# Which products of the second attention run as split fp32r, and which engine makes their weight remainders

## The chip, the cores and the metric

One core of one Trainium2 chip runs the whole program. The metric is the device time of one execution in microseconds; lower is better. The median of three runs of the kernel before is 2136.24 us (2134.52 to 2136.61).

## What is computed

The reference is a chain of two blocks on 256 tokens of width 1024, in fp32: a first block (sparse attention, latent attention, cross attention to a memory, a mixture of experts), then a second block of two layers. Layer 0 is a state-space mixer and a mixture of experts over the tokens and a context of 256 rows. Layer 1 is the part that is changed here and what follows it:

```python
h = rmsnorm(x, norm1_w) * (1 + sc1) + sh1          # tokens and context, each with its own scale and shift
q, k, v = split(h @ qkv_w)                          # 16 query heads, 4 key heads, 4 value heads of 64
q, k = rmsnorm per head, 2-D rotary embedding on the tokens
o = softmax(q @ concat(k_tokens, k_context).T / 8) @ v          # 256 x 1024
x = x + g1 * (o @ out_w)                                        # out_w is 1024 x 1024
x = x + g2 * moe_ec(rmsnorm(x, norm2_w) * (1 + sc2) + sh2)      # 16 experts, each takes 32 tokens; w1, w3, w2 are 1024 x 1024
return rmsnorm(x, final_norm_w)
```

The weights of the last mixture are 16 experts x 3 matrices x 4 MiB, 201 MB that are read from HBM once.

## The kernel before, in words

**Engines and queues.** Every engine has its own instruction stream, written out by hand in blocks (`@block.tensor`, `@block.scalar`, `@block.vector`, `@block.gpsimd`, `@block.sync`), and runs it strictly in order; they meet in semaphores (`wait_ge`, `then_inc`). The functions of one stage are five such lists. PSUM's eight banks are handed out in turn (`banks.open`); each bank is emptied by VectorE (`DVE`) or ScalarE (`ACTE`).

**Weights.** All weights come through a ring of pieces of 2 MiB (`weights`, `Ring`, `load_weights`). SBUF has seven slots (0 to 6) and some further rooms that are used in layer 1's mixture: the room of the queries and of `C` (slot number `SLOTS + 2`), an extra tile (`SLOTS + 1`), and the upper half of `hT` with another tile (`SLOTS + 3`). SyncE issues the loads in the order of the list, and before each it waits until the piece that held the slot before has been used (`before.freed`). `ring.add(name, slot, 0)` reserves a slot without a load: it is used for the rounded copy of a weight piece. The list order is: six pieces per expert of layer 0's mixture, the three pieces of the attention's qkv weight (`("qkv", 0..2)` in slots 6, 5, 4), the two pieces of its out-projection (slots 0 and 6), and six pieces per expert of layer 1's mixture in a cycle of ten places (line 378).

**Split products.** A plain fp32 matmul is exact enough but slow. `matmul_split` (lines 563 to 567) takes both operands as a sum of a rounded part (type fp32r) and a remainder, and issues three fp32r matmuls: high by low, high by high, low by high. The rounding is an ScalarE copy into an fp32r tile, the remainder a VectorE subtraction of the rounded tile from the original.

**The second attention (lines 3557 to 3800).** ScalarE rounds qkv piece 0, takes the squares of the four row tiles (two of context, two of tokens), rounds piece 1. GpSimd makes the four reciprocal roots, VectorE scales the rows, TensorE transposes them, and both VectorE and ScalarE evict the transposed rows into `hT` with scale and shift (`evict_h`). ScalarE then rounds `hT` into `h_high` in 16 parts of 256 columns, first the tokens' half, then the context's; VectorE makes the remainders `h_low` (`lower_h`) and those of the weights (`lower_w`), which go back into the slots of the raw weights. All three qkv pieces are multiplied as split products: pieces 0 and 1 for the queries (two row tiles each), piece 2 for keys and values (four row tiles). VectorE normalises and rotates the queries in four units (`QU`) and then the keys in four units, with reciprocal roots by GpSimd between; the remainders of piece 2 stand between the query units.

Then `PairAttention` (lines 982 to 1074) goes through eight pairs of heads, two steps each: TensorE the logits, VectorE the maximum, ScalarE the exponential with the sum, VectorE the scaling, TensorE the transposes, ScalarE their copies (`pT`), TensorE the products with the values (`pv`). VectorE copies each pair's output from PSUM into `oT` (line 1050). The out-projection (line 3657) is a plain fp32 matmul over `oT`, 32 products of 128 x 128 by 128 x 512, first the half `h = 0` of the weight for all four output tiles, then `h = 1`.

**The last mixture (`expert_choice(1)`).** After the norm and the routing, TensorE goes through the experts piece by piece (line 3217). A piece's place is free again when TensorE has used it; the piece ten places later in the list can then be loaded.

Of the kernel before, what the change touches and what calls it, by code (L numbers as in the profile page):

```python
# [5 lines left out]
F32 = mybir.dt.float32  # L6
# [175 lines left out]
def build(nc, A, out):  # L182
# [11 lines left out]
    with ctx:  # L194
# [183 lines left out]
        moe2_weights(1, (3, 5, 1, 4, SLOTS + 2, 2, SLOTS + 1, 0, 6, SLOTS + 3))  # L378
# [605 lines left out]
        class PairAttention:  # L984
# [4 lines left out]
            def __init__(self, tag, pairs, qT, kT, v, scale, outT, bufs):  # L989
                self.tag, self.steps, self.qT, self.kT, self.v = tag, 2 * pairs, qT, kT, v  # L990
                self.scale, self.outT = scale, outT
# [39 lines left out]
            def vector(self, dve, link):  # L1031
                for s in range(self.steps + self.LAG + 2):
# [13 lines left out]
                    p = self.done_pair(s - self.LAG - 1)  # L1046
                    if p is not None:
                        o = banks[self.tag, "pv", p]
                        dve.wait_ge(bank_full, o.full)
                        dve.tensor_copy(self.outT(p), o.ap[:, 0:S]).then_inc(emptied[DVE], 1)  # L1050

            def scalar(self, act):
                for s in range(self.steps + self.LAG):
                    if s < self.steps:
                        for i in (2 * s, 2 * s + 1):
                            act.wait_ge(self.max_ready, i + 1)
                            if i >= self.RING:
# [3 lines left out]
                                           accum_out=self.sums[:, i:i + 1]).then_inc(emptied[ACTE], 1)  # L1061
                    m = s - self.LAG
                    if m >= 0:
# [1992 lines left out]
        def expert_choice(l):  # L3056
# [11 lines left out]
            with ExitStack() as scope:  # L3068
# [41 lines left out]
                for n, piece in enumerate(PIECES):  # L3110
                    e, j = divmod(n, 6)
                    piece.freed = (half_used, 3 * e + j // 2 + 1) if j % 2 == 0 else ((h1_full, h3_full, y_full)[j // 2], e + 1)
                    if l == 0 and n % 8 == 7 or l == 1 and n % 10 == 6:
                        piece.ap = extra[0][:, :]
                    if l == 1 and n % 10 == 4:
# [440 lines left out]
        with ExitStack() as scope:  # L3556
# [3 lines left out]
            h_low = hT_r  # L3560
            h5_rounded, h5_split, w5_rounded, w5_split = (sem(x) for x in ("h5_rounded", "h5_split", "w5_rounded", "w5_split"))
            QKV = [(ring["qkv", n], ring["qkv_high", n]) for n in range(3)]
# [5 lines left out]
            early = ring["moe2", 1, 4]  # L3568
# [14 lines left out]
            oT = hflat[:, 0:2048].rearrange("p (k n) -> p k n", k=8)  # L3583
# [12 lines left out]
                                lambda p, kt: vv[:, kt, kv_of(p) * 64:(kv_of(p) + 1) * 64], HD ** -0.5, lambda p: oT[:, p, :], bufs)  # L3596
            block = whole

            def rounded_qkv(n, low=False):
                return rounded_slot(QKV[n][0 if low else 1].slot).rearrange("p (k n) -> p k n", k=KD)  # L3600

# [4 lines left out]
            def _(pe):  # L3606
                def product(tag, n, at, steps):
                    b = banks.open(tag, ACTE)
                    pe.wait_ge(*b.emptied)
                    for k in range(KD):  # L3610
                        if steps is not None:
                            pe.wait_ge(h5_split, steps + k)
# [237 lines left out]
```

## Time and profile before

| | |
|---|---|
| median of 3 runs | 2136.24 us |
| the profiled execution | 2135.01 us |
| its span (first to last instruction) | 2133.1 us |
| TensorE busy | 1980.8 us, 93% |
| VectorE / ScalarE / GpSimd busy | 952.6 / 682.2 / 98.1 us |
| DMA | 623.61 MB, mean 292 GB/s |
| granted TensorE clock | 0.982 of full speed, mean |

The profile is one execution. A plain fp32 matmul shows as two records of a matmul each, so 32 products are 64 records. "PE" is TensorE, "DVE" VectorE, "ACT" ScalarE, "POOL" GpSimd, "SPq" the queue of SyncE that issues the loads. A view of stages gives for each stretch how long every engine was busy; the chain of waits goes back from the last instruction to whatever released it and is printed in order of time; a timeline lists instructions of one engine, equal ones merged. Times are microseconds from the start of the span.

The attention of layer 1 lies between about 1503 and 1663 us, the last mixture behind it.

### The profile page before, as it was taken

What the parts mean: (1) busy time and instruction counts of PE and PEld (TensorE: products, weight loads), DVE (VectorE), ACT (ScalarE), POOL (GpSimd) and SP (SyncE); (2) the same over time, 40 slices, a digit from 0 to 9 for tenths busy, and PEclk for the clock granted to TensorE, in tenths of its full rate; (3) what the DMA queues carried; (4) which work ended last, traced back from release to release, by engine and by line L of the source; (5) the groups of instructions that cost most, each with busy time, mean ns of one, the idle gap of its engine ahead of it and who ended that gap; (6) DMA issues with size and microseconds to landing.
All of it is one profiled execution on the core that took longest, in us unless ns stands there. A gap on an engine that the chain in (4) does not pass through costs nothing.

```text
span 2133.1 us, 24870 instructions
## 1 busy us (share of the span) xinstructions
PE 1980.8 (93%) x10092; PEld 1088.3 (51%) x10092; DVE 952.6 (45%) x1702; ACT 682.2 (32%) x1326; POOL 98.1 (5%) x105
## 2 busy tenths in 40 slices
PE   8988988999899999999899999988899899999887
PEld 6845654444578888878533333322564433333222
DVE  5667425454887888853612222212875401111101
ACT  5254313111577776752311111100544211111001
POOL 0101000000101000100000000000210000000000
PEclk9989989999999999999999999999999999999999
DMA  9637778999044334325599999999641599999997
GB/s 368 218 126 276 285 290 319 383 404 334 25 141 119 100 118 144 113 73 218 206 422 428 427 427 428 427 427 426 262 183 60 216 418 425 428 426 426 426 427 323
DMA packets 143378, 623.61 MB, mean 292 GB/s; under 512 B 10976, under 2 KB 61280, under 8 KB 105376
## 3 DMA queue, kind: packets, MB, share of 16 engines
q1 hardware_dynamic: 141104, 618.83, 72.9%
q10 hardware_dynamic: 2160, 3.18, 0.4%
q8 instruction: 81, 1.33, 0.3%
q14 instruction: 33, 0.27, 0.0%
HBM read 620.80 MB, written 1.18 MB: 292 GB/s over the span
## 4 chain that ended last, share of the span: by engine, by line
PE 72%; DMA 14%; DVE 7%; ACT 3%; issue 2%; POOL 1%; SPq 1%; DVEq 0%; POOLq 0%; ACTq 0%
PE bank L3217 21%; PE bank L565 8%; PE bank L567 7%; PE bank L566 7%; DMA slots<-in_moe_w 7%; PE bank L1973 4%; DMA extra0e<-in_moe_w 3%; PE bank L635 2%; PE bank L3238 2%; PE bank L2000 2%; DMA hT<-in_moe_w 2%; PE bank L3188 2%; DMA spare_slot<-in_attn_qkv_w 2%; PE bank L2515 1%; PE bank L3657 1%
## 5 line engine op out<-in xcount | busy, mean ns | idle before, releaser
L3217 PE MATMUL bank<-slots,xgTe 128*64 128x512 f32 (+1 forms) x1408 | 315.6, 594 | 27.3 <-DMA slots<-in_moe_w 27.3
L3487 DVE TENSOR_TENSOR actse<-sge,bank 32x512 f32<-32x512 f32 (+1 forms) x48 | 32.8, 683 | 500.4 <-PE bank L3217 272.0
L3217 PEld LDWEIGHTS bank<-slots,xgTe 128*64 128x64 f32 (+1 forms) x1408 | 94.4, 124 | 229.2 <-issue 193.6
L3380 ACT ACTIVATE sge<-bank 32x512 f32<-32x512 f32 (+1 forms) x48 | 28.4, 591 | 461.2 <-PE bank L3217 461.0
L3217 PE MATMUL bank<-slots,aTe 128*64 128x512 f32 (+1 forms) x688 | 156.9, 601 | 13.6 <-issue 12.5
L566 PE MATMUL bank<-slots_r 128*128 128x512 f32 x416 | 163.4, 393 | 0.0
L565 PE MATMUL bank<-hT_r,slots_r 128*128 128x512 f32 x384 | 155.6, 405 | 0.0
L567 PE MATMUL bank<-slots_r 128*128 128x512 f32 x384 | 152.1, 396 | 0.0
L3392 ACT ACTIVATE aTe<-bank 128x512 f32<-128x512 f32 x32 | 19.1, 597 | 284.6 <-PE bank L3291 284.6
L2420 DVE TENSOR_TENSOR slots_r<-slots,slots_r 128x2048 fp32r<-128x2048 f32 x32 | 76.6, 2395 | 68.2 <-ACT slots_r L2415 68.1
L3217 PEld LDWEIGHTS bank<-slots,aTe 128*64 128x64 f32 (+1 forms) x688 | 49.8, 126 | 105.4 <-issue 103.1
L2792 DVE SCALAR_TENSOR_TENSOR slots<-slots,columns 128x512 f32<-128x512 f32 x128 | 98.7, 776 | 4.1 <-ACT slots L2637 0.3
L1973 PE MATMUL bank<-slots,hT 128*64 128x512 f32 x320 | 85.0, 595 | 4.9 <-ACT hT L2085 4.9
L566 PEld LDWEIGHTS bank<-slots_r 128*128 128x128 f32 x416 | 78.2, 188 | 18.3
L567 PEld LDWEIGHTS bank<-slots_r 128*128 128x128 f32 x384 | 72.2, 188 | 17.7
L565 PEld LDWEIGHTS bank<-hT_r,slots_r 128*128 128x128 f32 x384 | 72.1, 188 | 16.9 <-issue 1.2
L2415 ACT ACTIVATE slots_r<-slots 128x2048 fp32r<-128x2048 f32 x32 | 61.0, 1906 | 50.4 <-PE bank L567 50.4
L2654 ACT ACTIVATE rowsB<-rowsB,nb 128x128 f32<-128x128 f32 x256 | 76.4, 391 | 2.0 <-POOL rowsB L2617 2.0
L400 POOL TENSOR_SCALAR rstd<-eps_rows 128x1 f32<-128x1 f32 (+5 forms) x37 | 15.5, 418 | 1167.8 <-ACT xn L480 589.0
L565 PE MATMUL bank<-slots_r,hT_r 128*128 128x512 f32 (+1 forms) x176 | 68.2, 388 | 0.0
L3506 DVE TENSOR_TENSOR C<-C,bank 128x512 f32<-128x512 f32 x60 | 41.0, 684 | 60.6 <-PE bank L3238 60.6
L3493 DVE TENSOR_TENSOR ye0e<-bank,g2e 32x512 f32<-32x512 f32 (+1 forms) x24 | 16.5, 686 | 89.2 <-PE bank L3217 89.1
(633 smaller groups left out, 3471.6 us busy)
## 6 DMA issues: line engine op xcount, KB each, us to landing
slots<-in_moe_w SPq DMA_DIRECT2D x128, 2048.0 KB, 26.3
spare_slot<-in_moe_w SPq DMA_DIRECT2D x21, 2048.0 KB, 25.7
slots<-in_ada_w SPq DMA_DIRECT2D x20, 2048.0 KB, 10.9
extra0e<-in_moe_w SPq DMA_DIRECT2D x20, 2048.0 KB, 27.4
slots<-in_ssd_in_w SPq DMA_DIRECT2D x48, 512.0 KB, 5.3
slots<-in_moe_w_gate SPq DMA_DIRECT2D x20, 1024.0 KB, 9.0
slots<-in_moe_w_up SPq DMA_DIRECT2D x20, 1024.0 KB, 11.3
slots<-in_moe_w_down SPq DMA_DIRECT2D x19, 1024.0 KB, 15.2
```

The costliest lines, as they stand in the source:

```text
L565: pe.matmul(out, lhsT[0], rhs[1], start=start, stop=False, skip_group_check=True)
L566: pe.matmul(out, lhsT[0], rhs[0], start=False, stop=False, skip_group_check=True)
L567: return pe.matmul(out, lhsT[1], rhs[0], start=False, stop=stop, skip_group_check=True)
L635: i = pe.matmul(b.ap[:, 0:width], lhsT(k), rhs(k), start=(k == 0), stop=(k == K - 1))
L1973: i = pe.matmul(b.ap[j * CAP1:(j + 1) * CAP1, :].rearrange("p (m n) -> p m n", m=2), xg[:, p // 2 % 2, k, at:at + CAP1], piece.ap.rearrang ...
L2000: i = pe.matmul(b.ap[j * CAP1:(j + 1) * CAP1, :], aT[:, p % 2, f, j * CAP1:(j + 1) * CAP1], piece.ap[:, at:at + 512], start=(f == 0), stop ...
L2415: act.activation(high_half(w), raw_half(w), ACT.Copy).then_inc(w_rounded, 1)
L2420: dve.tensor_tensor(low_half(w), raw_half(w), high_half(w).bitcast(F32), ALU.subtract).then_inc(w_split, 1)
L2654: i = act.activation(r, r, ACT.Exp, bias=nb[:, t, col:col + 1])
L2792: i = dve.scalar_tensor_tensor(o, padded[:, c, :, j:j + S], tap(j, CH(g)[c]), o, ALU.mult, ALU.add)
L3188: i = pe.matmul(bank[:, u * W:(u + 1) * W], xn[:, j * NT + t, k * P:(k + 1) * P], onehot[:, t, j, g * W:(g + 1) * W], start=(t == 0), stop ...
L3217: i = pe.matmul(bank[64 * n:64 * n + NJ * CAP, :], lhsT(4 * h + k), wv[:, 0, n * 512:(n + 1) * 512], start=(h == 0 and k == 0), stop=(h == ...
```

## The change

The first query piece is multiplied in plain fp32: it needs neither a rounded copy nor remainders, and its products wait for the whole of `hT`. `h_high` and `h_low` are made afterwards in eight parts of 512 columns, tokens and context together; `h_low` moves from `hT_r` to slot 3. ScalarE's order is: the squares, half of piece 1, its evictions, the gate copies, the other half of piece 1, both halves of piece 2, `h_high`. VectorE makes the remainders of piece 1 and of `h`; those of piece 2 are made by GpSimd, ahead of the roots of the queries.

The out-projection becomes a split product. ScalarE rounds its weight in four halves of a piece (`round_out`, two behind the query copies, two between the key/value copies). GpSimd makes the four remainders, behind the roots of the keys in its list. In `PairAttention` ScalarE rounds each pair's output into `oT_high`, one step later than VectorE's copy stood, and VectorE subtracts it from PSUM into `oT_low`.

In the ring the places change: slots 1 and 2 hold the rounded pieces 1 and 2, slot 3 `h_low`, slots 5 and 1 the rounded halves of the out weight. The cycle of the last mixture starts with slots 4, 2, the queries' room, 3, the extra tile, 0, 5, 6, 1 and `SLOTS + 3`.

The diff, without the declarations of semaphores, without TensorE's part of the plain product and without the removed functions:

```diff
-            ring.add(("qkv_high", n), (3, 1, 2)[n], 0)
+            if n:
+                ring.add(("qkv_high", n), n, 0)
+        ring.add("h_low", 3, 0)
+        for n in range(2):
...
-        moe2_weights(1, (3, 5, 1, 4, SLOTS + 2, 2, SLOTS + 1, 0, 6, SLOTS + 3))
+        moe2_weights(1, (4, 2, SLOTS + 2, 3, SLOTS + 1, 0, 5, 6, 1, SLOTS + 3))
...
-                    p = self.done_pair(s - self.LAG - 1)
+                    p = self.done_pair(s - self.LAG - 2)
                     if p is not None:
-                        o = banks[self.tag, "pv", p]
-                        dve.wait_ge(bank_full, o.full)
-                        dve.tensor_copy(self.outT(p), o.ap[:, 0:S]).then_inc(emptied[DVE], 1)
+                        dve.wait_ge(self.out_rounded, self.rounded_from + p + 1)
+                        dve.tensor_tensor(self.out_low(p), banks[self.tag, "pv", p].ap[:, 0:S],
+                                          self.out_high(p).bitcast(F32), ALU.subtract).then_inc(emptied[DVE], 1)
...
-                for s in range(self.steps + self.LAG):
+                for s in range(self.steps + self.LAG + 2):
...
+                    p = self.done_pair(s - self.LAG - 2)
+                    if p is not None:
+                        o = banks[self.tag, "pv", p]
+                        act.wait_ge(bank_full, o.full)
+                        act.activation(self.out_high(p), o.ap[:, 0:S], ACT.Copy).then_inc(self.out_rounded, 1)
...
-            h_low = hT_r
+            h_low = rounded_slot(3).rearrange("p (k n) -> p k n", k=KD)
...
+                pe.wait_ge(lowered5, 2 + KD)
+                for t in range(NT):
+                    product(("q5", 1, t), 1, S + t * P)
+                pe.wait_ge(lowered5_pool, 2)
                 for t in range(TT):
-                    product(("kv5", t), 2, t * P, KD + 1 if t == 0 else None)
+                    product(("kv5", t), 2, t * P)
                 pe.wait_ge(q_ready, 1)
...
-                    w = ring["attn_out", h]
+                    pe.wait_ge(lowered5_pool, 4 + 2 * h)
                     for t, n, b in outs:
                         if h == 0:
                             pe.wait_ge(*b.emptied)
                         for k in range(4):
-                            i = pe.matmul(b.ap[:, :], oT[:, 4 * h + k, t * P:(t + 1) * P], wv[:, k, n * 512:(n + 1) * 512],
-                                          start=(h == 0 and k == 0), stop=(h == 1 and k == 3), skip_group_check=True)
+                            tt, c = slice(t * P, (t + 1) * P), slice(n * 512, (n + 1) * 512)
+                            i = matmul_split(pe, b.ap[:, :], (oT_high[:, 4 * h + k, tt], oT_low[:, 4 * h + k, tt]),
+                                             (rounded_out(h)[:, k, c], rounded_out(h, True)[:, k, c]),
+                                             h == 0 and k == 0, h == 1 and k == 3)
                         if h == 1:
...
+                for j in range(2):
+                    pool.wait_ge(rounded5, 3 + j)
+                    c = slice(4 * j, 4 * j + 4)
+                    pool.tensor_tensor(rounded_qkv(2, True)[:, c, :], raw_qkv(2)[:, c, :],
+                                       rounded_qkv(2)[:, c, :].bitcast(F32), ALU.subtract).then_inc(lowered5_pool, 1)
                 qn.pool(pool)
                 kn.pool(pool)
+                for h in range(2):
+                    for j in range(2):
+                        pool.wait_ge(rounded5, 5 + KD + 2 * h + j)
+                        c = slice(2 * j, 2 * j + 2)
+                        pool.tensor_tensor(rounded_out(h, True)[:, c, :], view(OUT[h][0], 0, 4, D)[:, c, :],
+                                           rounded_out(h)[:, c, :].bitcast(F32), ALU.subtract).then_inc(lowered5_pool, 1)
...
+                norm.scalar_squares(act, added)
+                round_w(1, 0)
+                for k in range(1, KD, 2):
+                    evict_h(act, ACTE, k)
+                for n in range(2):
+                    copy_out(act, ACTE, ("g15", 0, n), g1[:, n * 512:(n + 1) * 512], 512)
+                round_w(1, 1)
+                round_w(2, 0)
+                round_w(2, 1)
+                act.wait_ge(bank_full, banks["n5", KD - 1].full)
+                for k in range(KD):
                     b = banks["n5", k]
                     act.wait_ge(emptied[b.by], b.done)
...
+                    act.activation(h_high[:, k, :], hT[:, k, :], ACT.Copy).then_inc(rounded5, 1)
                 for n in range(2):
                     for t in range(NT):
...
+                def round_out(h, j):
+                    raw, high = OUT[h]
+                    act.wait_ge(raw.sem, raw.full)
+                    act.wait_ge(*high.before.freed)
+                    c = slice(2 * j, 2 * j + 2)
+                    act.activation(rounded_out(h)[:, c, :], view(raw, 0, 4, D)[:, c, :], ACT.Copy).then_inc(rounded5, 1)
+
+                round_out(0, 0)
+                round_out(0, 1)
                 for t in range(TT):
...
+                    if t < 2:
+                        round_out(1, t)
...
+                for j in range(2):
+                    dve.wait_ge(rounded5, j + 1)
+                    c = slice(4 * j, 4 * j + 4)
+                    dve.tensor_tensor(rounded_qkv(1, True)[:, c, :], raw_qkv(1)[:, c, :],
+                                      rounded_qkv(1)[:, c, :].bitcast(F32), ALU.subtract).then_inc(lowered5, 1)
+                dve.wait_ge(*ring["h_low"].before.freed)
                 for k in range(KD):
-                    lower_h(k, 1)
+                    dve.wait_ge(rounded5, 4 + k + 1)
+                    dve.tensor_tensor(h_low[:, k, :], hT[:, k, :], h_high[:, k, :].bitcast(F32),
+                                      ALU.subtract).then_inc(lowered5, 1)
```

## Rows read from the trace of the kernel before

**Rows 1.** Stages: length, busy us of PE, PEld, DVE, ACT, POOL, clock, DMA share, GB/s.

```profile
1542.00:1571.60 29.60, 26.77 (x117) 21.24 (x115) 21.17 (x51) 3.83 (x10) 9.08 (x11) 0.94 0.44 168
1587.00:1634.90 47.90, 43.40 (x288) 25.14 (x286) 37.32 (x111) 33.95 (x80) 0.00 (x0) 1.00 0.00 1
1683.00:1941.00 258.00, 249.09 (x1180) 88.23 (x1180) 29.57 (x48) 35.39 (x86) 0.00 (x0) 1.00 0.97 410
```

**Rows 2.** Chain of waits in order of time (start, us, what), near the end.

```profile
1949.77 41.34 DMA hT<-in_moe_w
```

**Rows 3.** Timeline of the queue that issues the weight loads (start, us, what).

```profile
1662.69 0.33 SPq L392 DMA_DIRECT2D spare_slot<-in_moe_w  x1
1672.01 0.43 SPq L392 DMA_DIRECT2D hT<-in_moe_w  x1
1690.23 12.01 SPq L392 DMA_DIRECT2D slots<-in_moe_w  x4
```

**Rows 4.** Chain of waits, ahead of the products.

```profile
1502.70 3.71 ACT slots_r L3689 x2
1507.84 2.45 POOL rstd L401
1513.97 0.75 DVE xn L497
```

**Rows 5.** Timeline of GpSimd in the attention.

```profile
1510.57 0.93 POOL L401 TENSOR_TENSOR rstd<-rstd,minus_half 128x1 f32<-128x1 f32 x1
1572.04 1.05 POOL L401 TENSOR_TENSOR rstd<-rstd,minus_half 128x4 f32<-128x4 f32 x1
1658.90 0.58 POOL L401 TENSOR_TENSOR rstd<-rstd,minus_half 128x1 f32<-128x1 f32 x1
```

**Rows 6.** Chain of waits, the out-projection.

```profile
1634.92 27.75 PE bank L3657 x64
```

**Rows 7.** Timeline of ScalarE in the attention.

```profile
1523.99 2.59 ACT L3695 ACTIVATE h_high<-hT 128x256 fp32r<-128x256 f32 x8
1553.15 0.39 ACT L3720 ACTIVATE k<-bank 128x256 f32<-128x256 f32 x1 [9.65 <-PE bank L567]
1558.75 0.39 ACT L3720 ACTIVATE k<-bank 128x256 f32<-128x256 f32 x1 [4.94 <-PE bank L567]
1594.25 1.08 ACT L1071 ACTIVATE hT<-bank 128x512 f32<-128x512 f32 x2
```

**Rows 8.** The loads of the two qkv pieces in the ring slots, by tile.

```profile
L392 SPq DMA_DIRECT2D slots<-in_attn_qkv_w x2: 5346/13164/20983, 1472.4 to 1493.4; - x2
...
DMA to landing us min/median/max: 20.1/34.9/35.7
```

**Rows 9.** Timeline of VectorE in the attention.

```profile
1505.17 2.47 DVE L3526 TENSOR_TENSOR X<-X,bank 128x512 f32<-128x512 f32 x4
1527.99 2.77 DVE L3734 TENSOR_TENSOR hT_r<-hT,h_high 128x256 fp32r<-128x256 f32 x8
1543.36 2.29 DVE L3740 TENSOR_TENSOR slots_r<-slots,slots_r 128x2048 fp32r<-128x2048 f32 x1
1573.56 0.43 DVE L735 TENSOR_TENSOR k<-k,rstd 128x256 f32<-128x256 f32 x1
1581.30 0.49 DVE L1045 TENSOR_SCALAR probs<-probs,sums 128x512 f32<-128x512 f32 x1
```

**Rows 10.** Duration ns min/median/max: GpSimd's select and a VectorE operation.

```profile
L2617 POOL TENSOR_SCALAR_AFFINE_SELECT rowsB<-rowsB x16: 2007/2010/3522, 605.0 to 906.7; 128x2048 f32<-128x2048 f32 x16
...
L2792 DVE SCALAR_TENSOR_TENSOR slots<-slots,columns x128: 737/752/2383, 577.8 to 894.5; 128x512 f32<-128x512 f32 x128
```

**Rows 11.** Timelines of VectorE and GpSimd around 607 us, first layer 0.

```profile
605.53 2.38 DVE L2792 SCALAR_TENSOR_TENSOR slots<-slots,columns 128x512 f32<-128x512 f32 x1
...
607.33 2.45 POOL L2617 TENSOR_SCALAR_AFFINE_SELECT rowsB<-rowsB 128x2048 f32<-128x2048 f32 x1
```

**Rows 12.** Chain of waits, a value product in the pair loop.

```profile
1595.49 1.92 PE bank L1026 x16
```

More of the change, by code:

```diff
@@ L987, in build, with __init__ @@
             RING, LAG = 6, 2
-            def __init__(self, tag, pairs, qT, kT, v, scale, outT, bufs):
+            def __init__(self, tag, pairs, qT, kT, v, scale, out, bufs):
                 self.tag, self.steps, self.qT, self.kT, self.v = tag, 2 * pairs, qT, kT, v
-                self.scale, self.outT = scale, outT
+                self.scale = scale
+                self.out_high, self.out_low, self.out_rounded, self.rounded_from = out
                 self.probs, self.pT, self.negmax, self.sums = bufs
@@ L3559, in build @@
             h_high = nc.alloc_sbuf_tensor_at("h_high5", [P, KD, 2 * S], F32R, offset=shared_at)
-            h_low = hT_r
-            h5_rounded, h5_split, w5_rounded, w5_split = (sem(x) for x in ("h5_rounded", "h5_split", "w5_rounded", "w5_split"))
-            QKV = [(ring["qkv", n], ring["qkv_high", n]) for n in range(3)]
+            h_low = rounded_slot(3).rearrange("p (k n) -> p k n", k=KD)
+            rounded5, lowered5, lowered5_pool = (sem(x) for x in ("rounded5", "lowered5", "lowered5_pool"))
+            QKV = {n: (ring["qkv", n], ring["qkv_high", n]) for n in (1, 2)}
             kk = sb("k5", [P, TT, KVH * 64], scope=scope)
@@ L3600, in rounded_qkv, with rounded_out @@
                 return rounded_slot(QKV[n][0 if low else 1].slot).rearrange("p (k n) -> p k n", k=KD)
+            OUT = [(ring["attn_out", h], ring["out_high", h]) for h in range(2)]
+            def rounded_out(h, low=False):
+                return rounded_slot(OUT[h][0 if low else 1].slot).rearrange("p (k n) -> p k n", k=4)
             def raw_qkv(n):
@@ L3606, in _, with product @@
             def _(pe):
-                def product(tag, n, at, steps):
+                def product(tag, n, at):
                     b = banks.open(tag, ACTE)
@@ L3610, in product @@
                     for k in range(KD):
-                        if steps is not None:
-                            pe.wait_ge(h5_split, steps + k)
                         c = slice(at, at + P)
@@ L3621, in _ @@
                 gate_banks(pe, "g15", 1, 2, 0, ACTE)
-                for n in range(2):
-                    pe.wait_ge(w5_split, 2 * n + 2)
-                    for t in range(NT):
-                        product(("q5", n, t), n, S + t * P, 1 if (n, t) == (0, 0) else None)
-                pe.wait_ge(w5_split, 6)
+                for k in range(KD):
+                    norm.wait_chunk(pe, k)
+                piece = ring["qkv", 0]
+                pe.wait_ge(piece.sem, piece.full)
+                wv = view(piece, 0, KD, 512)
+                for t in range(NT):
+                    b, _ = gemm(pe, ("q5", 0, t), lambda k: hT[:, k, S + t * P:S + (t + 1) * P], KD, t,
+                                lambda k: wv[:, k, :], 512, ACTE)
+                piece.freed = (bank_full, b.full)
+                pe.wait_ge(lowered5, 2 + KD)
+                for t in range(NT):
+                    product(("q5", 1, t), 1, S + t * P)
+                pe.wait_ge(lowered5_pool, 2)
                 for t in range(TT):
-                    product(("kv5", t), 2, t * P, KD + 1 if t == 0 else None)
+                    product(("kv5", t), 2, t * P)
                 pe.wait_ge(q_ready, 1)
@@ L3662, in _ @@
                         i.then_inc(half_out, 1)
-                ring["attn_out", 0].freed, ring["attn_out", 1].freed = (half_out, 1), (bank_full, b.full)
+                for h, last in enumerate(((half_out, 1), (bank_full, b.full))):
+                    OUT[h][0].freed = OUT[h][1].freed = last
             def evict_h(eng, by, k):
```

68 lines of the change are left out of this document (14 added, 54 removed).

## The prediction, made before the result was known

> **What bounds the kernel now.** I read three views. First the stages: the last one, the second mixture of experts, has the DMA engines at 97% of its first 258 us and 410 GB/s [rows 1]. The chain of waits confirms who is late there: near the end TensorE sits up to 41 us in a wait for one weight piece [rows 2]. The DMA queue shows where that stream starts. Of the experts' pieces, number 8 is issued at 1662.69 (out-projection done) and 9 at 1672.01; the next, at 1690.23, waits for TensorE's first use of a piece [rows 3]. From there the stream never pauses, so the end lies a fixed distance behind 1690.23, and that lies 27.5 us behind the end of the out-projection. Hence the rule I use: each microsecond by which the second attention ends earlier or later moves the end by one.
>
> Inside the attention I followed the chain: ACT rounds a weight piece before it squares (1502.70, 3.71 us), a GpSimd root takes 2.45 us, the last scaling stands at 1513.97 [rows 4]. Then come the products, the key chain, eight head pairs and the out-projection. In the pair loop TensorE is 43.4 of 47.9 us busy, VectorE 37.3 and ScalarE 34.0 [rows 1]: a loop of three engines, none with much to give.
>
> **Front, up to the products.** ACT no longer rounds ahead of the squares; it starts with the first finished rows, about 1504.1, against 1506.4 (1502.70 + 3.71). The 2.45 us root becomes an ordinary one, since VectorE's weight subtraction beside it goes: such a root takes 0.58 alone and 0.93 beside a scaling on VectorE [rows 5]. The adds that feed the last square end at 1507.6 (1505.17 + 2.47) [rows 9], two per row tile of 0.6 each, so the first tile was ready 3.6 earlier; square 1.2, root 0.9 and 0.3, so the last scaling starts at 1510.0 in place of 1513.97. Transposes and eight evictions (about 1.0 us for two on ACT) end near 1515.3.
>
> The first query piece in plain fp32: 16 products. The out-projection's 32 take 27.75 us, 0.867 each [rows 6], so 13.9 us: 1515.4 to 1529.3. A split group of 8 products takes 5.60 us (copies at 1553.15 and 1558.75) [rows 7], so 16 took 11.2: the plain ones lose 2.7 and start 4.7 earlier.
>
> Beside that ACT does its half of piece 1, two gate copies, then three halves of 1.86 us [half of rows 4's 3.71], each 128x2048, ending 1518.3, 1520.2, 1522.1. Piece 1 lands at 1472.4 + 35.7 = 1508.1 and piece 2 at 1493.4 + 20.1 = 1513.5 [rows 8], so neither waits. Then 8 roundings of 128x512: 128x256 costs 0.324 (8 in 2.59) and 128x2048 1.86, so 0.54 by interpolation, until 1526.4. VectorE follows with 0.61 each (from 2.77 for 8 and 2.29) [rows 7, 9]: alone it would be done at 1527.6, before TensorE asks.
>
> **It is not alone: the price of the GpSimd subtractions.** Nothing in this trace is a wide two-input GpSimd operation. Lower bound: its one-input select over 128x2048, 2.01 us at best [rows 10]. Upper bound: three times that, 6.0, if each of its two reads and its write went at the select's whole time. I take twice the select, 4.0 us, as two tiles are read for one; each 0.5 us more adds 1.0, 0.5 and 1.5 us to the three collisions below. The Trainium skill (GPSIMD Engine Reference, "Elementwise — side-by-side cycle accounting") has 4497 ns for a 128x2048 fp32 tensor_tensor on GpSimd; no run here shows it, and the sum below by it would be +9.0 in place of +5.9.
>
> The trace shows what such an operation does to VectorE. At 605 a VectorE operation with two SBUF inputs, median 0.75 us, takes 2.38 beside the two selects, and the second select 2.45 [rows 10, 11]: they exclude each other for a whole instruction and alternate. The power at 1507.84, 2.45 us beside a VectorE subtraction [rows 4], and the 0.93 against 0.58 beside a one-input scaling [rows 5], say the same from the other side. The Trainium skill (SBUF — State Buffer, "SBUF: two separate sides") gives this as a rule, an exclusive lock on a shared port pair against VectorE's two-port modes and two-SBUF-input operations; the trace agrees.
>
> Three places collide:
> 1. Front. GpSimd gets the port at 1520.7 (after VectorE's last piece-1 subtraction), until 1524.7. The first h remainder runs to 1525.3, GpSimd until 1529.3, then seven remainders of 0.61: 1533.6. TensorE, ready at 1529.3, starts at 1533.7 and its clock has fallen: before, a gap of 3 us ahead of the kv products made the first take 7.4 us (1545.7 to 1553.1) in place of 5.6, with granted clock 0.94 over that stage [rows 1, 7]. So 1533.7 + 11.2 + 1.8 + 22.4 = 1569.1, against 1569.7: **-0.6**.
> 2. Key chain. The first out-weight subtraction stands directly behind the last key root (1572.04, 1.05 us), long satisfied; VectorE's last key scaling, two SBUF inputs, comes 0.4 us later at 1573.56 [rows 5, 9] and is on the path. It waits for nearly all of it: **+3.8**.
> 3. First probabilities. Three subtractions are left; by 4.0 each they end at about 1581, 1585 and 1589.6. The first two scalings of probabilities (before: from 1581.30 [rows 9], now due at 1584.5) fall on the last two: 0.7 + 4.0, less 0.6 of slack of VectorE per pair: **+4.1**.
>
> **The pair loop.** VectorE's copy becomes a subtraction from PSUM, both about 0.42 us, no change. ScalarE gets one 128x256 rounding per pair, 0.28 to 0.4, between its exponentials and its pT copies. Those copies start at 1594.25, take 1.08 and end 0.16 us before the value product at 1595.49 [rows 7, 12]: no cover. Bounds 0 (if VectorE alone paces the loop) and 0.4; I take 0.3 x 7 = 2.1, and 0.4 at the end, where rounding and subtraction follow each other ahead of the out-projection: **+2.5**.
>
> **Clock.** Stalls 2 and 3 each let TensorE idle over 4 us. Between 0 and 1.8 each, mostly in a stretch where it is not alone the bound: **+1.5** for both.
>
> **Out-projection.** 32 products at 0.70 (5.60/8) in place of 0.867: 22.4 for 27.75, **-5.35**. Its GpSimd remainders are ready 40 us before.
>
> **Ring order.** By the end of the last value product seven pieces of the experts could be asked for, now five; pieces 5 and 6 come at half the out-projection, 7 and 8 at its end, 9 at about 9 us later. A piece takes 4.9 us (2.1 MB at the 427 GB/s of the page's slices): the last lands some 17 us after the out-projection, and piece 10 is asked for 27.5 us after it: **0**; cover gone, it would cost up to 9.8. The moves past SP's queue add no wait of their own: no slot is asked for before attention's own loads.
>
> Sum: -0.6 + 3.8 + 4.1 + 2.5 + 1.5 - 5.35 = +5.95. The profiled execution took 2135.01 (span 2133.1); 2141.0. It stands 1.2 below the median of the three runs, so I say **2142.2**.
>
> **Rivals.**
> - A, faster: GpSimd's subtraction is short. By 2.0 us: front 1529.6, no cold clock, kv products end at 1563.2 (-6.5), keys +1.9, probabilities 0, loop +2.5, out-projection -5.35: -7.4, 2128.8. If it did not exclude VectorE at all, -9.5: 2126.7. By 3.0 us it is -2.9; it decides at about 3.4 us. For it: the selects, 2.01. Against it: two inputs.
> - B, no difference: exclusion as forecast, but collision 3 misses (the scalings fall behind the last subtraction) and ScalarE's rounding finds slack: 4 to 6 us less, 2136 to 2138.
> - C, much slower: the prefetch is short of two pieces when the experts start, +9.8: 2152. Against it: the 10 us of margin above.
> - D, the subtraction is longer than twice a select, up to the three of the upper bound, or the clock is cold after every stall: 3 us for each 0.5, so +9 at one half more and +12 at one (2145 to 2148); the whole bound would give +18, 2154, where the later scalings no longer all collide.
>
> **How the numbers follow.** A change of under 0.2% (4.3 us, 2132.0 to 2140.5) can't be told from none. Forecast (2140 to 2145) 0.38; D 0.22; A 0.2; B 0.15; C 0.05. Slower: most of the forecast, D and C: 0.62; same: B, the forecast's low edge and A's high one: 0.2; faster 0.18. The range drops C, the far end of D and half of A: 2128.5 to 2150.
>
> **What would show it.** GpSimd rows of 128x2048 at 4 us or more; VectorE's h remainder, last key scaling and first two probability scalings lengthened to several microseconds; a gap on TensorE between the plain and the split query products; the out-projection in 22.4 us. A TensorE without that gap, or a key scaling of 0.43, makes it wrong.

## The result, and the profile after

| | median us (runs) | lowest to highest | ratio to before, 95% interval |
|---|---|---|---|
| before | 2136.11 (12) | 2133.82 to 2138.02 | 1 |
| after | 2141.38 (12) | 2139.93 to 2148.44 | 1.0030 [1.0022, 1.0038] |

Forecast: 2142.2, slower. The medians lie 5.3 us apart. The profiled execution of the changed kernel took 2141.71 us, its span 2139.8 (before 2133.1), so its span grew by 6.7.

The stages come first, in the columns of [rows 1]; the first line is the gap on TensorE, the second the key chain, the third the last mixture.

```profile
1529.30:1534.20 4.90, 0.60 (x3) 0.01 (x1) 4.90 (x8) 0.60 (x1) 0.67 (x1) 0.80 0.64 200
1570.00:1587.00 17.00, 7.90 (x86) 6.56 (x85) 14.08 (x15) 4.33 (x7) 14.99 (x5) 0.79 0.94 381
1690.00:1948.00 258.00, 249.08 (x1182) 88.18 (x1182) 29.44 (x47) 35.45 (x87) 0.00 (x0) 1.00 0.97 410
```

The kernel before, over the same stretch as the key chain's line:

```profile
1570.00:1587.00 17.00, 13.22 (x114) 9.23 (x114) 14.24 (x41) 10.86 (x24) 1.38 (x2) 0.90 0.92 372
```

The last mixture is what it was [rows 1]: 410 GB/s, DMA share 0.97, TensorE busy 249.08 for 249.09. The time must have come from ahead of it, as the timeline of the queue that issues the weight loads confirms:

```profile
1669.55 0.33 SPq L396 DMA_DIRECT2D spare_slot<-in_moe_w  x1
...
1697.11 0.33 SPq L396 DMA_DIRECT2D slots<-in_moe_w  x1
```

The end of the out-projection moved from 1662.69 to 1669.55 (+6.86), piece 10 from 1690.23 to 1697.11 (+6.88) [rows 3], the span by 6.7. The rule "one microsecond of the attention moves the end by one" held for this pair of executions, and the new order of the ring cost nothing.

GpSimd's timeline, to be read beside [rows 5]:

```profile
1520.21 9.77 POOL L3705 TENSOR_TENSOR slots_r<-slots,slots_r 128x2048 fp32r<-128x2048 f32 x2 [9.72 <-ACT slots_r L3723]
1572.34 1.05 POOL L405 TENSOR_TENSOR rstd<-rstd,minus_half 128x4 f32<-128x4 f32 x1
1573.37 9.07 POOL L3713 TENSOR_TENSOR slots_r<-slots,slots_r 128x2048 fp32r<-128x2048 f32 x2
1582.41 9.15 POOL L3713 TENSOR_TENSOR spare_slot_r<-spare_slot,slots_r 128x2048 fp32r<-128x2048 f32 x2
```

The pair at 1573.37 and the pair at 1582.41 make four subtractions of 4.5 to 4.6 us each, where I had taken 4.0 as twice the select [rows 10]. The Trainium skill (GPSIMD Engine Reference, "Elementwise — side-by-side cycle accounting") gives 4497 ns; the trace agrees.

VectorE's timeline, to be read beside [rows 9]:

```profile
1522.55 7.98 DVE L3779 TENSOR_TENSOR slots_r<-hT,h_high 128x512 fp32r<-128x512 f32 x2 [1.89 <-ACT h_high L3738]
1573.67 4.36 DVE L738 TENSOR_SCALAR rstd<-rstd 128x4 f32<-128x4 f32 x1
1578.06 4.67 DVE L739 TENSOR_TENSOR k<-k,rstd 128x256 f32<-128x256 f32 x1
1582.88 1.29 DVE L610 COPY xn<-bank 128x512 f32<-128x512 f32 x2
1587.90 0.69 DVE L1043 TENSOR_REDUCE negmax<-bank 128x1 f32<-128x512 f32 x1 [2.55 <-PE bank L1012]
1588.63 0.15 DVE L1044 TENSOR_SCALAR negmax<-negmax 128x1 f32<-128x1 f32 x1
1591.38 0.49 DVE L1050 TENSOR_SCALAR probs<-probs,sums 128x512 f32<-128x512 f32 x1
```

And two more lines of VectorE from the kernel before:

```profile
1573.36 0.17 DVE L734 TENSOR_SCALAR rstd<-rstd 128x4 f32<-128x4 f32 x1
...
1577.96 0.69 DVE L1038 TENSOR_REDUCE negmax<-bank 128x1 f32<-128x512 f32 x1 [1.34 <-PE bank L1007]
```

Two subtractions of h that cost 0.6 each take 7.98 together, the key scaling 4.67 in place of 0.43 [rows 9]. The line between shows what I had missed: the multiplication of four numbers per partition by a constant ahead of it, at 1573.67, takes 4.36, where it took 0.17 before. Beside the long subtractions GpSimd and VectorE go in turn, one instruction each: each of VectorE's two ends just behind one of GpSimd's. What reads a PSUM bank (the copies of 1.29 for two, the reduction of 0.69) or is 128x1 keeps its time beside the same subtractions. The first scaling of probabilities stands at 1591.38, GpSimd's last subtraction ends at 1591.56, 0.18 us later, and the scaling takes its usual 0.49: that collision did not happen.

The chain of waits, in order of time (start, us, what):

```profile
1522.55 11.60 DVE slots_r L3779 x8
1534.19 0.80 PE bank L569
...
1611.53 0.36 DVE h_high L1054
1611.89 0.04 issue
1611.94 0.66 PE bank L1021 x4
1612.60 1.90 PE bank L1031 x16
...
1619.50 1.90 PE bank L1031 x16
...
1645.96 0.39 ACT hT_r L1071
1646.37 0.44 DVE h_high L1054
1646.85 0.51 PE bank L569
```

A value product of the kernel before, in its chain of waits, one pair behind that of [rows 12]:

```profile
1602.13 1.92 PE bank L1026 x16
```

TensorE waits for the eighth remainder of h until 1534.19. In the loop the chain passes through VectorE's new subtraction, behind which TensorE's transposes wait, and value products follow each other every 6.91 us (1612.60, 1619.50), against 6.64 before (1595.49, 1602.13). The out-projection takes 1669.55 - 1646.85 = 22.70 for 27.75 [rows 6].

### The profile page after: what moved, and what is told of

It reads as the page before. It is cut to its first block, busy times and chain, and to the rows that moved or that the text cites. A ratio compares the mean times of both kernels' runs of the same rounds, so it can differ in the third digit from the quotient of the medians.

```text
span 2139.8 us, 24908 instructions
## 1 busy us (share of the span) xinstructions
PE 1980.5 (93%) x10108; PEld 1091.5 (51%) x10108; DVE 957.8 (45%) x1690; ACT 687.5 (32%) x1328; POOL 124.1 (6%) x111
## 4 chain that ended last, share of the span: by engine, by line
PE 71%; DMA 14%; DVE 8%; ACT 3%; issue 2%; POOL 1%; SPq 1%; DVEq 0%; POOLq 0%; ACTq 0%
PE bank L3227 21%; DMA slots<-in_moe_w 10%; PE bank L569 8%; PE bank L571 8%; PE bank L570 8%; PE bank L1983 4%; PE bank L639 2%; PE bank L3248 2%; DMA C<-in_moe_w 2%; PE bank L2010 2%; DMA hT<-in_moe_w 2%; PE bank L3198 2%; PE bank L2525 1%; PE bank L1113 1%; PE bank L1967 1%
## 5 line engine op out<-in xcount | busy, mean ns | idle before, releaser
L571 PE MATMUL bank<-slots_r 128*128 128x512 f32 x432 | 171.6, 397 | 0.0
L570 PE MATMUL bank<-slots_r 128*128 128x512 f32 x416 | 163.4, 393 | 0.0
L571 PEld LDWEIGHTS bank<-slots_r 128*128 128x128 f32 x432 | 81.7, 189 | 20.2
L570 PEld LDWEIGHTS bank<-slots_r 128*128 128x128 f32 x416 | 78.2, 188 | 18.3
L569 PE MATMUL bank<-slots_r,hT_r 128*128 128x512 f32 (+1 forms) x192 | 74.7, 389 | 0.9 <-DVE h_high L1054 0.9
```

Of the source, the lines that this page charges most:

```text
L569: pe.matmul(out, lhsT[0], rhs[1], start=start, stop=False, skip_group_check=True)
L570: pe.matmul(out, lhsT[0], rhs[0], start=False, stop=False, skip_group_check=True)
L571: return pe.matmul(out, lhsT[1], rhs[0], start=False, stop=stop, skip_group_check=True)
```

## Experiments

Each was timed against the kernel before in rounds of its own session (5 to 11 runs of each experiment), and its ratio is to the kernel before of that session, whose median was 2135.96 to 2136.43. The code is shortened to the lines that carry the change. "Attention" is the time from the first addition of the last rows to the end of the out-projection in the profiled execution: it leaves out small shifts that a run has brought along from earlier. Runs of one kernel lie up to 4 us apart for before (2133.82 to 2138.02) and up to 8.5 for after (2139.93 to 2148.44), so the traces are the sharper judge of a single step.

| | attention us | median us | ratio, 95% interval |
|---|---|---|---|
| before | 159.92 | 2136.11 | 1 |
| after | 166.90 | 2141.38 | 1.0030 [1.0022, 1.0038] |
| 1 plain out-projection | 160.60 | 2134.95 | 0.9995 [0.9986, 1.0004] |
| 2 piece 2 by VectorE | 160.13 | 2136.60 | 0.9998 [0.9989, 1.0007] |
| 3 GpSimd waits for the keys | 166.32 | 2143.89 | 1.0038 [1.0025, 1.0052] |
| 4 no remainders of the out weights | 156.73 | 2134.39 | 0.9990 [0.9981, 0.9999] |
| 5 VectorE rounds in the loop | 165.43 | 2141.65 | 1.0024 [1.0015, 1.0033] |
| 6 sixteen pieces, one a step | 161.96 | 2138.30 | 1.0011 [1.0002, 1.0020] |
| 7 sixteen pieces, at once | 163.75 | 2139.37 | 1.0018 [1.0009, 1.0027] |
| 8 = 2 + 5 + 6 | 153.78 | 2128.95 | 0.9970 [0.9958, 0.9982] |
| 9 = 8, pieces placed | 149.00 | 2126.99 | 0.9955 [0.9941, 0.9969] |
| 10 = 2, plain out-projection, no GpSimd | 153.76 | 2129.43 | 0.9964 [0.9950, 0.9977] |

Theory: GpSimd's subtraction holds off VectorE's instructions with SBUF operands, one for one, and this costs more than the out-projection gives. Rival one: the ring's new order, or the split as such, costs the time. Rival two: the instructions that were added to VectorE and ScalarE do.

**1. The out-projection's part undone, the ring's order kept.**

```
-  dve.tensor_tensor(self.out_low(p), ...)          # and act's rounding, the weights' rounding,
-  pool.tensor_tensor(rounded_out(h, True) ...)     # GpSimd's four subtractions, the split products
+  dve.tensor_copy(self.outT(p), o.ap[:, 0:S]).then_inc(emptied[DVE], 1)
```

> The changed kernel with the whole out-projection part undone (plain fp32 product, VectorE's copy, no rounding, no GpSimd remainders of the out weight), but its ring order and places kept. Exclusion theory (GpSimd's wide subtraction and VectorE's operations on SBUF shut each other out for a whole instruction): only the front collision is left; the kv products end where they did before (1570.0 against 1569.7 us), keys and pair loop are those of before: 2136.4, within 1.5 us of before. Rival, the prefetch is what costs (five expert pieces ahead in place of seven): the ring is unchanged here, so it stays at about 2141.

2134.95: no different from before, and the ring is the changed one. The expectation (2136.4, within 1.5) holds, and the ring as the cause falls.

**2. The remainders of piece 2 by VectorE.**

```
-  pool.tensor_tensor(rounded_qkv(2, True)[:, c, :], ...)
+  dve.tensor_tensor(rounded_qkv(2, True)[:, c, :], ...).then_inc(lowered5, 1)   # behind h's remainders
```

> The changed kernel with the remainders of qkv piece 2 made by VectorE behind its h remainders, none by GpSimd there. Exclusion theory: the eight h remainders take 4.9 us in place of 11.6, TensorE goes from the plain to the split query products at 1529.3 without a gap and without a fall of its clock, the kv products end at 1562.9, 7.1 us earlier; the key collision stays 8.7 us: 2134.3. Rival (the h remainders are late because of ScalarE's order, not GpSimd): gap unchanged, 2141 or more, as VectorE has 4.6 us more to do.

ScalarE's copies of the products (each stands at the end of a product group), then VectorE, in their timelines:

```profile
1527.74 0.60 ACT L652 ACTIVATE q<-bank 128x512 f32<-128x512 f32 x1 [3.36 <-PE bank L639]
1533.35 0.60 ACT L652 ACTIVATE q<-bank 128x512 f32<-128x512 f32 x1 [5.00 <-PE bank L571]
```

```profile
1520.37 4.90 DVE L3774 TENSOR_TENSOR slots_r<-hT,h_high 128x512 fp32r<-128x512 f32 x8 [1.90 <-ACT h_high L3733]
1525.19 4.48 DVE L3778 TENSOR_TENSOR slots_r<-slots,slots_r 128x2048 fp32r<-128x2048 f32 x2
1564.74 4.35 DVE L738 TENSOR_SCALAR rstd<-rstd 128x4 f32<-128x4 f32 x1
1569.13 4.67 DVE L739 TENSOR_TENSOR k<-k,rstd 128x256 f32<-128x256 f32 x1
```

VectorE has 4.48 us more work and is done earlier: eight remainders of h in 4.90 us for 11.59. The copies are 5.61 apart (after: 12.35, 1529.92 to 1542.27), the attention 6.8 shorter. So the gap was the collision with GpSimd and not VectorE's load; rival two falls in the front. The key chain is blocked as in the changed kernel (4.35, 4.67). The median, 2136.60, is 4.8 below that of the changed kernel and 2.3 above the expectation of 2134.3.

**3. GpSimd waits until the keys are scaled.**

```
+  pool.wait_ge(k_ready, TT)        # ahead of the four subtractions
```

> The changed kernel, with GpSimd's four out-weight remainders held back by one wait until the last key is scaled. Exclusion theory: the keys are free (-8.7, and -1 for a less cold clock), but the four subtractions now end about 4.5, 9, 13.5 and 18 us behind the last key, where VectorE has its first scalings of probabilities: three of these wait 1.7, 4.6 and 3 us, some 8.5 in all. So the time stays: 2140, within 2 us of the changed kernel's 2141.4. Rival (only what stands directly behind a root is hurt, the pair loop has slack for it): 2131.6, as without the remainders.

GpSimd's timeline, then VectorE's:

```profile
1575.66 8.98 POOL L3714 TENSOR_TENSOR slots_r<-slots,slots_r 128x2048 fp32r<-128x2048 f32 x2 [1.04 <-DVEq L3801]
1584.60 9.33 POOL L3714 TENSOR_TENSOR spare_slot_r<-spare_slot,slots_r 128x2048 fp32r<-128x2048 f32 x2
```

```profile
1575.10 0.42 DVE L739 TENSOR_TENSOR k<-k,rstd 128x256 f32<-128x256 f32 x1
1582.83 2.08 DVE L1050 TENSOR_SCALAR probs<-probs,sums 128x512 f32<-128x512 f32 x1
1585.03 4.54 DVE L1050 TENSOR_SCALAR probs<-probs,sums 128x512 f32<-128x512 f32 x1
1591.24 2.97 DVE L1050 TENSOR_SCALAR probs<-probs,sums 128x512 f32<-128x512 f32 x1
```

The key chain is free, and three scalings of probabilities (0.49 each when free) take 8.1 more instead, for the 8.5 expected. The price moved; the attention is 0.6 shorter. The third collision of my forecast is real where the schedule brings it about. The time was a miss: 2143.89, 2.5 above the changed kernel where I had allowed 2. In the profiled executions it was not lost in the attention: 1.2 of it lies ahead of it and 3.2 behind, in two falls of the clock that experiments 4 and 5 describe.

**4. No remainders of the out weights.** The products that should use them take the rounded weights again, so the output lacks what the remainders add and holds a wrong term in its place. It is a kernel for timing only; TensorE's work is the same.

```
-  pool.tensor_tensor(rounded_out(h, True)[:, c, :], ...)      # all four
-  (rounded_out(h)[:, k, c], rounded_out(h, True)[:, k, c])
+  (rounded_out(h)[:, k, c], rounded_out(h)[:, k, c])
```

> The changed kernel without the remainders of the out weight: GpSimd makes none, and the product that should use the remainder takes the rounded weight again, so TensorE's work is the same. Exclusion theory: the last key's root scaling and key scaling go back from 4.36 and 4.67 us to 0.17 and 0.43 (-8.7), and the first logits find a less cold clock (-1): 2131.6. Rival (pair loop and cold clock of a late start are the cost, not the collision): no more than 2 us faster, 2139.5.

VectorE's timeline:

```profile
1574.48 0.17 DVE L738 TENSOR_SCALAR rstd<-rstd 128x4 f32<-128x4 f32 x1
1574.69 0.42 DVE L739 TENSOR_TENSOR k<-k,rstd 128x256 f32<-128x256 f32 x1
1579.08 0.69 DVE L1043 TENSOR_REDUCE negmax<-bank 128x1 f32<-128x512 f32 x1 [1.34 <-PE bank L1012]
```

The two scalings are back at 0.17 and 0.42 (8.4 less), the logits behind them run at full clock (1.2 less), and the attention is 10.2 shorter. The last 0.6 is not the subtractions' price: it lies in the front, where nothing was changed and the first split products ran at a granted clock of 0.77 for 0.70. The median went down by 7.0, and the expectation (2131.6) is missed by 2.8: the profiled execution gave back 1.4 ahead of the attention and 1.6 behind piece 10, places where nothing was changed. The second of these is the clock: a run of 64 products just behind piece 10 takes 15.62 us here and 13.93 in after, with the granted clock at 0.66 in 1703 to 1708 (after, at the same place: 1.00). Before, after and experiments 1, 2, 5 and 6 have 13.93; 3, 4, 7, 8, 9 and 10 have 15.62.

**5. VectorE rounds and subtracts in the pair loop.**

```
-  act.activation(self.out_high(p), o.ap[:, 0:S], ACT.Copy)
+  link(dve.tensor_copy(self.out_high(p), o.ap[:, 0:S]))       # ahead of the subtraction
```

> The changed kernel, but in the pair loop VectorE makes both the rounded copy and the remainder, at the place where the copy stood before (in its wait behind the value product); ScalarE does nothing new. If the 0.28 us per pair (6.91 against 6.63) come from ScalarE's rounding and from the PSUM bank that is held until the late subtraction: period back at 6.63, -1.9 and -0.3 at the end: 2139.2. Rival: VectorE is the pace and 0.42 us more per pair shows: 2141 to 2144.

The chain of waits:

```profile
1604.00 1.92 PE bank L1031 x16
...
1610.63 1.92 PE bank L1031 x16
...
1686.58 5.47 PE bank L3195 x32
```

The period is 6.63 again. VectorE has 0.42 more work per pair and the loop is the faster for it: VectorE's load is not what cost, and of rival two ScalarE's added rounding is left. Two things went at once, and the experiment does not part them. One is the subtraction that comes late and holds the bank of the value product until then: in the changed kernel VectorE reaches it at 1611.53, in its own order behind two scalings, and TensorE's next transposes wait for it. The other is ScalarE's rounding ahead of its copies of the transposes, which the value product needs as well. In the changed kernel's timeline of ScalarE:

```profile
1611.05 0.37 ACT L1071 ACTIVATE hT_r<-bank 128x256 fp32r<-128x256 f32 x1
1611.32 1.08 ACT L1081 ACTIVATE pT<-bank 128x512 f32<-128x512 f32 x2
```

The copies start 0.27 later for the rounding and end at 1612.40, 0.20 ahead of the value product at 1612.60. Before they ended 0.16 ahead of it [rows 7, 12]. So without the late subtraction the copies would have held the product nearly as long.

The attention gained 1.5, the median nothing (2141.65 for an expected 2139.2, which is a miss and inside the rival's range): in the profiled execution the 32 products at 1686.58 took 5.47 where after has 3.84 for them, with the granted clock at 0.87 in 1687 to 1700 (after: 1.00), and piece 10 came 29.1 us behind the out-projection in place of 27.6. Experiments 3, 6, 7 and 9 had the same: 5.43 to 5.47 for these products, clock 0.87, piece 10 29.2 us behind; 1, 2, 4, 8 and 10 had 3.84, 1.00 and 27.4 to 27.7. All these are of one profiled execution per kernel. What sends the clock down there was not tried.

**6. Sixteen subtractions of 128x512, one for each step of the pair loop,** released when the step's logits are in their bank. A step is half a pair: one set of logits, its reductions and two scalings.

```
+  for s_ in range(16):
+      pool.wait_ge(bank_full, banks["att5", "qk", 2 * s_].full)
+      pool.tensor_tensor(... [:, k, c] of 128x512 ...)
```

> The changed kernel, with the out-weight remainders cut into 16 subtractions of 128x512, one in each step of the pair loop, released when that step's first logits are full; VectorE then has 1.6 us of work on PSUM (two maxima) before it touches SBUF again. Exclusion theory with a hold of one instruction: a subtraction takes 1.2 us, fits into that window, and costs nothing: 2131.6, as without the remainders. Rival (any wide work of GpSimd slows the pair loop, whatever its place): period of a pair above 6.91 by 0.5 or more, 2136 or more.

GpSimd, then VectorE:

```profile
1601.94 1.27 POOL L3713 TENSOR_TENSOR slots_r<-slots,slots_r 128x512 fp32r<-128x512 f32 x1 [4.41 <-PE bank L1012]
1604.02 1.27 POOL L3713 TENSOR_TENSOR spare_slot_r<-spare_slot,slots_r 128x512 fp32r<-128x512 f32 x1 [0.82 <-PE bank L1012]
```

```profile
1603.60 0.49 DVE L1050 TENSOR_SCALAR probs<-probs,sums 128x512 f32<-128x512 f32 x1
1604.20 1.38 DVE L1050 TENSOR_SCALAR probs<-probs,sums 128x512 f32<-128x512 f32 x1
```

A miss: 2138.3 for 2131.6. The key chain is free, but TensorE computes a pair's two sets of logits 2.08 us apart, ahead of VectorE, so every second piece starts just before a scaling and makes it 1.38. The pairs are 7.76 apart for 6.91: 0.9 us of wait in each. The time and the period are those of the rival; experiment 9 tells the two apart.

**7. The same sixteen, released at once behind the last key root.**

```
+  for s_ in range(16):
+      pool.tensor_tensor(... [:, k, c] of 128x512 ...)        # no wait on the logits
```

> The same 16 subtractions of 128x512, but one behind the other straight behind the last key root, as in the changed kernel. Exclusion theory: the wait of each blocked VectorE instruction is one GpSimd instruction, so the last root scaling and key scaling wait 1.2 us each in place of 4.2 (-6.3); the other fourteen run on for some 17 us and hold up four to six scalings of probabilities by up to 1.2 each (+4): 2138 to 2139. Rival (the port goes over only when GpSimd's list is empty): no change against the changed kernel, 2141.4.

VectorE:

```profile
1572.11 1.12 DVE L738 TENSOR_SCALAR rstd<-rstd 128x4 f32<-128x4 f32 x1
1573.27 1.44 DVE L739 TENSOR_TENSOR k<-k,rstd 128x256 f32<-128x256 f32 x1
```

The price of a wait follows the length of the other engine's instruction: 2.0 us over both where the long ones cost 8.4. So 6.4 should come back, and 3.2 did: the pieces run on to 1592.7 and meet four scalings of probabilities, which take 3.1 more. 2139.37, just above the expected 2138 to 2139; the rival's 2141.4 lies within the spread of the runs (2136.99 to 2142.53), but the rows rule it out.

**8. Experiments 2, 5 and 6 in one.**

> All three remedies together: piece 2's remainders by VectorE, the out-weight remainders as 16 subtractions in step with the pair loop, rounded copy and remainder of each pair's output both by VectorE. Exclusion theory, from the kernel before: kv products end 6.8 earlier, keys and pair loop as before (+0.4 at its end), out-projection 5.0 shorter: -11.4, 2124.8. Rival (what is won ahead of the last mixture is lost again, as its weights can't be asked for earlier): the sum is cut, 2130 or more.

2128.95, faster than before, but 4.2 above the expectation, mainly for the cause found in 6: pairs 7.49 apart, in most of them one scaling at 1.38. The attention is 6.1 shorter than before's, where 11.4 was expected.

**9. As 8, with the pieces placed behind VectorE's own progress:** five behind the last key scaling, where VectorE reads PSUM only, each of the others behind the second scaling of a step, where reductions from PSUM follow.

```
-  pool.wait_ge(bank_full, banks["att5", "qk", 2 * s_].full)
+  if n == 0: pool.wait_ge(k_ready, TT)
+  if n >= 5: pool.wait_ge(att.scaled, 2 * (n - 4))            # counts scalings of probabilities
```

> As the kernel with all three remedies, but the 16 subtractions of 128x512 are released by VectorE's own progress, not by the logits: five of them behind the last key (7 us in which VectorE only empties PSUM), the others each when VectorE has done both scalings of a step, where two maxima over PSUM follow. There the last release came too early in every second step and one scaling took 1.38 us in place of 0.49: period 7.49. Exclusion theory: here no scaling is lengthened, the period is 6.63, and the pair loop gives back 6 us: 2123 to 2125. Rival (GpSimd beside the loop costs 0.8 a pair wherever it starts): 2129, as there.

GpSimd, then VectorE:

```profile
1567.60 6.18 POOL L3708 TENSOR_TENSOR slots_r<-slots,slots_r 128x512 fp32r<-128x512 f32 x5 [1.10 <-DVEq L3799]
1575.87 1.26 POOL L3708 TENSOR_TENSOR slots_r<-slots,slots_r 128x512 fp32r<-128x512 f32 x1 [2.08 <-DVE probs L1050]
```

```profile
1574.71 0.49 DVE L1050 TENSOR_SCALAR probs<-probs,sums 128x512 f32<-128x512 f32 x1
...
1575.70 0.68 DVE L1043 TENSOR_REDUCE negmax<-bank 128x1 f32<-128x512 f32 x1
```

Every scaling is back at 0.49, the reduction beside a piece stays at 0.68, the pairs are 6.64 apart, and the attention is 4.8 shorter than in 8 by the placing alone. 2126.99, ratio 0.9955 [0.9941, 0.9969]: the fastest of all, with the same products, roundings and remainders as the changed kernel, some of them on other engines. It is 2.0 above the upper end of the expectation (2123 to 2125); its profiled execution had both falls of the clock, 1.6 and 1.7 us.

**10. The front of 9 alone:** no work for GpSimd, the out-projection in plain fp32.

> Only the front of the change, without GpSimd: first query piece in plain fp32, the new order of the rounding, piece 2's remainders by VectorE; the out-projection plain and VectorE's copy as before. Theory: kv products end 6.8 earlier, all behind that is as before: 2129.3. With the kernel above the difference is what the split out-projection is worth when nothing collides: 5.0 less 0.4 at the end of the pair loop. Rival (the last mixture does not follow the attention's end one to one): 2132 or more.

2129.43, as expected. The front is worth 6.2 in the attention (159.92 - 153.76; 6.8 expected), the split out-projection without collisions 4.8 more (153.76 - 149.00). In the times the second step shows as 2.4, and the intervals of the two overlap, so only the traces show it; 1.7 of the difference is the slower clock of the fetch, which this run did not have (27.5 us from the out-projection to piece 10, 29.2 in 9).

## Why the prediction was right, and where it was not

| step | forecast | measured |
|---|---|---|
| front | -0.6 | +0.3 |
| key chain | +3.8 | +8.4 |
| first probabilities | +4.1 | 0 |
| clock | +1.5 | +1.2 |
| pair loop and its end | +2.5 | +2.0 |
| out-projection | -5.35 | -5.05 |
| ring | 0 | 0 |
| sum | +5.95 | +6.9 |

**What bounds the kernel.** The step held, but one row under it was misread. The 41.34 us in [rows 2] is the way of one piece from its issue to its landing, which the chain follows; TensorE was busy for 35.41 of them. Its longest single wait for a weight behind piece 10 is 2.2 us.

**Front.** ScalarE copies the last keys at 1570.27, 0.3 later than before (1569.96). By my working with 4.5 us for the subtraction the last keys would have come 0.4 later. TensorE started the split products at 1534.19, forecast 1533.7, and the first group of eight took 8.1 us in place of 5.6, where I had allowed 1.8 for the clock; experiment 2 shows the cause of the gap.

**Key chain and first probabilities: this is the step that failed, and two errors cancelled.** "It waits for nearly all of it: +3.8" counted one instruction, the scaling of the keys. The multiplication ahead of it, 128x4, is blocked as well: (4.36 - 0.17) + (4.67 - 0.43) = 8.4. By that second wait the probabilities come so late that GpSimd is done 0.18 us behind the start of the first scaling, which is not lengthened, and the +4.1 falls away. Forecast for both 7.9, measured 8.4. Experiment 3 shows the same 8 us in the other place. With the 4.5 us known and the collisions still counted wrongly my sum was +9.0; so the total came out well for 4.0 us partly by luck. Counted right, at 4.5 us each, it is 0.3 + 8.4 + 1.2 + 2.0 - 5.05 = 6.85.

**Clock.** Of the 9.94 by which the first reduction of logits is late (1577.96 to 1587.90), the front explains 0.3 and the waits 8.4; 1.2 is left for the transposes and first logits, with the granted clock at 0.79 over 1570 to 1587 (before 0.90 over the same stretch). In 1583 to 1588, behind the wait, it was 0.50, the lower of the clock's two levels; before had 1.00 over the same work (1573.9 to 1577.96). It came once, not for two stalls.

**Pair loop.** From the first reduction to the out-projection it is 58.95 for 56.96. The size was forecast. I had ScalarE's copies of the probabilities later by a rounding; the chain shows TensorE waiting for the late subtraction, which I had at nothing. The rows give both nearly the same length (the copies end 0.20 ahead of the value product), and experiment 5, which brings the period back, takes both away. Which of them alone would cost the 0.27 us of a pair stays open.

**Out-projection.** 22.70 in place of 22.4 for 32 products. The first matmul took 0.51 us where those behind it took 0.39 to 0.40; no row shown here says where the rest of the 0.3 lies.

**Rivals.** A needed a subtraction under 3.4 us: it was 4.5. (By the prediction's own 3 us for each 0.5 the turn would lie at 3.0; it changes nothing here.) Half of B's condition came true (the scalings fell behind the last subtraction); its other half did not, as the pair loop still cost 2.0, and its time did not come, since the key chain had taken the price. C had its 10 us of margin. D's half microsecond came (4.5 for 4.0), but not its +3: both collisions of the out-projection's subtractions that I had priced at 9.9 for 4.5 us cost 8.4.

## What to carry to other kernels

Count an operation given to GpSimd by what it blocks: here each VectorE instruction beside it that had two SBUF inputs, or went from SBUF to SBUF over more than one element per partition (128x4, 128x512), could pay up to one whole GpSimd instruction, however small it was itself; look above all for chains of small ones. Cut such an operation into short pieces, and release each by VectorE's own progress, ahead of work that reads PSUM: from 8 to 9 the placing alone took 4.8 us out of the attention. Together with piece 2's remainders and the rounding of the outputs moved to VectorE it turned +7.0 into -10.9 us. Look for the engine that can free a bank first, even where that engine is the busier one: the pair loop lost 0.27 us a pair with the freeing put one step later and the rounding on ScalarE.

## What the runs showed of the hardware

- A VectorE multiplication of 128x4 from SBUF to SBUF takes 4.36 us beside GpSimd's subtraction (0.17 alone), one of 128x1 keeps its 0.15. The Trainium skill (VectorE: DVE Perf Modes, "Mode 2×_2P — use both read ports for one tensor") has an operation with one SBUF source take both ports where its outermost non-unit dimension is even; both rows agree, and I had read over this for so small an operation.
- GpSimd's subtraction of 128x512 takes 1.27 us, of 128x2048 4.5 us: in pieces the same work costs 0.5 to 0.6 us more per 128x2048.
- The granted clock fell in the fetch of the last mixture (0.87 for 1.00 over 13 us, 1.6 us of time: 5.47 for 3.84 on 32 products) in the profiled executions of five of the ten experiments, and just behind piece 10 (15.62 for 13.93 on 64 products) in those of six; the code there is the same as in the others. Why stays open. Two such falls are as large as several of the steps measured here, so a difference of 3 us between medians can't be put down to the attention without a trace.
